# Prompt attention on TensorE: score products placed ahead of and between the groups of turned probabilities

## The reference, cut to what matters

```python
def diff_attn_prompt(q, k, v, lam):
    ...
        p1 = jax.nn.softmax(jnp.where(causal, jnp.einsum('bqhd,bkhd->bhqk', qb[..., :HEAD_DIM], k1), NEG), axis=-1)
        p2 = jax.nn.softmax(jnp.where(causal, jnp.einsum('bqhd,bkhd->bhqk', qb[..., HEAD_DIM:], k2), NEG), axis=-1)
        return jnp.einsum('bhqk,bkhd->bqhd', p1 - lam * p2, vf)
```

## Time and profile before

| | before |
|---|---|
| median of 3 runs | 2821.29 us |
| profiled execution, its own time | 2816.94 us |
| its span, first to last instruction | 2814.8 us |
| TensorE busy (matmul), whole span | 2492.6 us, 89% |
| DVE, ACT, POOL busy, whole span | 42%, 24%, 5% |
| mean granted TensorE clock | 0.942 of full |

### The profile page before, as it was taken

The page is one execution under the profiler, slowest core; times in us unless marked ns, Lnnn a source line. Parts: engine busy times, 40 slices in busy tenths (PEclk is TensorE's granted clock), DMA queues, the critical chain, the costliest instruction groups (busy, mean ns, idle before and its releaser), DMA issues.

```text
span 2814.8 us, 39064 instructions
## 1 busy us (share of the span) xinstructions
PE 2492.6 (89%) x15803; PEld 2277.5 (81%) x15803; DVE 1170.6 (42%) x2316; ACT 669.6 (24%) x1160; POOL 153.5 (5%) x186
## 2 busy tenths in 40 slices
PE   3999967778887798999999999944899999999997
PEld 2878845545554798999999999934899999999996
DVE  5312044445577561333333333499233333333225
ACT  5212122235565231111111111123211111111112
POOL 0011100014432000000000000000000000000000
PEclk6999988899998899999999999967999999999998
DMA  2322267773353100111111111011011111111001
GB/s 95 137 77 73 107 225 298 268 255 126 121 194 127 60 31 31 46 46 46 45 45 45 45 45 45 15 38 38 31 46 46 46 46 45 46 46 45 31 23 64
DMA packets 118794, 227.60 MB, mean 81 GB/s; under 512 B 6675, under 2 KB 81732, under 8 KB 116099
## 3 DMA queue, kind: packets, MB, share of 16 engines
q1 hardware_dynamic: 113267, 178.67, 18.7%
q0 software_dynamic: 5392, 46.96, 4.8%
HBM read 207.49 MB, written 51.41 MB: 92 GB/s over the span
## 4 chain that ended last, share of the span: by engine, by line
PE 77%; DVE 8%; issue 8%; ACT 2%; DMA 2%; SPq 2%; POOL 1%; DVEq 0%; ACTq 0%
PE ps L1562 69%; DMA kraw<-cache_win_k_a 2%; PE ps L1628 2%; PE ps L656 1%; PE ps L637 1%; PE ps L622 1%; ACT sm L551 1%; SPq L726 1%; DVE orms L1369 1%; POOL sm L864 1%; DVE rstd L1197 1%; DVE pa L1506 1%; SPq L723 1%; DVE sm L496 1%; PE ps L1642 1%
## 5 line engine op out<-in xcount | busy, mean ns | idle before, releaser
L1562 PE MATMUL ps<-xn,ws 128*128 128x384 f32 (+1 forms) x6912 | 1171.2, 331 | 90.0 <-issue 39.9
L1562 PEld LDWEIGHTS ps<-xn,ws 128*128 128x128 f32 x6912 | 1164.4, 191 | 95.9 <-issue 58.0
L1562 PE MATMUL ps<-hh,ws 128*128 128x384 f32 (+1 forms) x3168 | 533.9, 329 | 8.7 <-issue 8.7
L1562 PEld LDWEIGHTS ps<-hh,ws 128*128 128x128 f32 x3168 | 529.4, 189 | 9.2 <-issue 9.2
L1403 DVE TENSOR_TENSOR act_h<-act_s,ps 128x384 f32<-128x384 f32 x132 | 70.2, 532 | 901.0 <-ACT act_s L1043 901.0
L1390 DVE TENSOR_TENSOR x<-ps,x 128x384 f32<-128x384 f32 (+1 forms) x552 | 284.8, 533 | 190.8 <-PE ps L1562 189.1
L1043 ACT ACTIVATE act_s<-ps 128x384 f32<-128x384 f32 x132 | 62.5, 473 | 1261.1 <-PE ps L1562 1145.9
L1562 PE MATMUL ps<-wp,xn 128*128 128x512 f32 (+1 forms) x1296 | 297.3, 392 | 18.8 <-DVE xn L1210 18.8
L1562 PEld LDWEIGHTS ps<-wp,xn 128*128 128x128 f32 (+1 forms) x1296 | 237.5, 183 | 79.0 <-issue 19.7
L1329 DVE TENSOR_TENSOR ws<-wraw,ws 128x2048 fp32r<-128x2048 f32 x70 | 159.6, 2283 | 7.1 <-ACT ws L998 7.1
L1628 PE MATMUL ps<-ident,kraw 128*128 128x128 f32 x512 | 91.4, 333 | 60.4 <-DMA kraw<-cache_win_k_a 34.0
(11 more groups left out here) (178 smaller groups left out, 1449.0 us busy)
## 6 DMA issues: line engine op xcount, KB each, us to landing
wraw<-w_gate SPq DMA_DIRECT2D x22, 1024.0 KB, 5.2
wraw<-w_up SPq DMA_DIRECT2D x22, 1024.0 KB, 5.2
wraw<-w_down SPq DMA_DIRECT2D x22, 1024.0 KB, 4.8
kraw<-cache_win_k_a SPq DMA_DIRECT2D x8, 2048.0 KB, 8.0
vraw<-cache_win_v_a SPq DMA_DIRECT2D x8, 2048.0 KB, 11.4
kraw<-cache_k_b SPq DMA_DIRECT2D x64, 256.0 KB, 11.3
vraw<-cache_v_b SPq DMA_DIRECT2D x64, 256.0 KB, 4.2
o_wk_s<-cache_win_k_a POOLq DMA_DIRECT2D x8, 2032.0 KB, 9.0
```

The source lines that it names most:

```text
L1562: r = mm(out, w(a), m(b_), start=(i == 0 and q_ == 0), stop=(i == n - 1 and q_ == 2))
```

## The change

`scores` and `turn_p` now take a list of what to do, and the loop over the steps on TensorE puts a unit's first two score products (the first 512 keys, both halves) ahead of the turned groups, and the other two, where there are any, behind the first group (`mix` 1) or the first two groups (`mix` 0). The waits within stay as they are, and go along with what they guard. Nothing changes on the other engines.

```diff
-            def scores(u):
+            def score_pieces(u):
+
+                return [(c0, s) for c0 in range(0, unit_at(u)[3], 512) for s in range(2)]
+
+            def scores(u, pieces):
 
                 pair, mix, i, n = unit_at(u)
-                if i == 0:
+                if not pieces:
+                    return
+                if i == 0 and pieces[0] == (0, 0):
                     for part in range(2):
                         pe.wait_ge(qk_ready[part], 2 * pair + 2)
                 masked_before = 8 * pair + (0, 0, 1, 2, 4, 5, 6, 7)[i]
                 if masked_before:
                     pe.wait_ge(scores_masked, 2 * masked_before)
...
-                q_.then_inc(scores_done, 1)
-
-            def turn_p(u):
+                if pieces[-1] == score_pieces(u)[-1]:
+                    q_.then_inc(scores_done, 1)
+
+            def turn_p(u, groups):
...
-                for s, k0, cnt in turn_groups(u):
+                for s, k0, cnt in groups:
...
             for step in range(UNITS + VALUE_LAG):
+                pieces = score_pieces(step) if step < UNITS else []
+                scores(step, pieces[:2])
                 if 0 <= step - TURN_LAG < UNITS:
-                    turn_p(step - TURN_LAG)
-                if step < UNITS:
-                    scores(step)
-                    if next_round(step):
-                        turn_qk(*next_round(step))
+                    u = step - TURN_LAG
+                    groups = turn_groups(u)
+                    first = 1 if unit_at(u)[1] else 2
+                    turn_p(u, groups[:first])
+                    scores(step, pieces[2:])
+                    if groups[first:]:
+                        turn_p(u, groups[first:])
+                else:
+                    scores(step, pieces[2:])
+                if step < UNITS and next_round(step):
+                    turn_qk(*next_round(step))
```

More of the change, by code:

```diff
@@ L617, in scores @@
                     pe.wait_ge(scores_masked, 2 * masked_before)
-                for c0 in range(0, n, 512):
+                for c0, s in pieces:
                     w = min(512, n - c0)
[L620 to L623, removed]
-                q_.then_inc(scores_done, 1)
-            def turn_p(u):
+                    rows = head_rows(s)
+                    q_ = mm(ps[:, score_bank(i, s) + c0 // 512, 0:w], qk[rows, pair % 2, 0, i * P:(i + 1) * P],
+                            qk[rows, pair % 2, 1, c0:c0 + w], start=True, stop=True)
+                if pieces[-1] == score_pieces(u)[-1]:
+                    q_.then_inc(scores_done, 1)
+            def turn_p(u, groups):
                 pair, mix, i, n = unit_at(u)
```

## The result

The changed kernel has a median of 2789.81 us over 4 runs (2784.56 to 2793.64), the kernel before 2820.84 us in the same session (4 runs, 2819.74 to 2822.61). The ratio is 0.9888, with a 95% interval of 0.9871 to 0.9905: faster by 31 us, 1.1%. The forecast was 2822.3 us in a range from 2814 to 2831, so the result lies outside of it. The profiled execution took 2784.56 us, with a span of 2782.5 us and a mean granted clock of 0.954 (before 2816.94, 2814.8 and 0.942).

A forecast was written before the change was run, and what follows sets the result against it. TensorE's waits in the 287.1 us stage, for banks and masks, and its half clock were taken as the bound. +5.7 - 1.6 - 0.8 - 2.3 = +1.0 on 2816.94, plus 4.35 to the median: 2822.3 us, range 2814 to 2831.

The forecast's parts named there:

- Outside it nothing moves: Whole kernel: only the 287.1 us stage that the change touches was taken to change in time.
- Part 1, last pair: Blocks 4 to 7: 13 turned blocks and four splits inside the mask loop add 2.7 us, bounds 1.4 to 3.3.
- Part 2, pairs 4 to 6: Mix 1 pairs: +0.9 us in pairs 5 and 6, +0.3 in pair 4, and +0.3 more for each of three.
- Part 3, mix 0 pairs: Pairs 0 to 3: bank waits exchanged for mask waits, -0.4 us a pair, -1.6 for four, bounds -3 and +2.
- The mask loop: Rival, chance 0.25: the loop of scores and masks binds mix 0 pairs too, +1.3 us each, 2831.4 us in all.
- The start: First pair's start, where a block waited 2.3 us for q's copy: 0.8 us less.
- Part 4, clock: Stage: stretches at half clock fall from eight to six, -2.3 us, bounds -9.2 and +1.2.
- clock kept: Rival, chance 0.15: half-clock stretches vanish and mix 0 pairs take the better account, -7.3 us, 2814.0 us.
- A mean clock of 0.99 in the stage: Sign named against the forecast: the stage's mean granted clock, 0.95 before, goes to 0.99.
- The price of a stretch: Stage: each half-clock stretch was taken to cost 1.15 us, from a range of 0.6 to 1.4.
- slow stretches follow the long waits: Stage: half clock follows TensorE waits of 1.84, 2.06 us and the like, or two waits close together.
- The exchange of waits: Stage, chance 0.60: turned blocks' waits for q and k copies nearly vanish; scores' mask waits grow from 8.3 to over 25 us.

The follow-up runs named there:

- e1: Kernel before plus four one-column matmuls (16 TensorE instructions) in idle time ahead of layer 1's feed-forward loop, attention unchanged; 2800.44 us, ratio 0.993.
- e2: Changed kernel plus 60 one-column matmuls (240 instructions) ahead of layer 1's loop, which then stands 256 instructions behind its place before; 2815.39 us, ratio 0.9978.
- e3: Against the kernel before, all of a unit's scores ahead of all its turned groups, none between; no padding; 2806.08 us (one run).
- e6: Kernel before with all of a unit's scores ahead of its turned groups, plus 16 TensorE instructions ahead of layer 1's loop; 2786.44 us, ratio 0.9878.
- e7: Kernel before plus 32 one-column matmuls (128 TensorE instructions) ahead of layer 1's loop; 2801.46 us (one run).
- e9: Changed order in pairs 0 to 3, order of before in pairs 4 to 7, plus 16 instructions ahead of layer 1's loop; 2792.26 us (one run).
- e10: Changed kernel plus 16 TensorE instructions ahead of layer 1's loop; 2792.32 us (one run).
- e11: Changed order in pairs 0 to 3, order of before in pairs 4 to 7, plus 32 instructions ahead of layer 1's loop; 2796.71 us (one run).
- e8: Kernel before plus one one-column matmul (4 TensorE instructions) ahead of layer 1's loop; 2803.07 us (one run).
- e5: Against the changed kernel, a unit's scores whole, behind its first turned group (one or two groups, or mix 1) or second (four groups); 2762.62 us, ratio 0.9798.
- e4: Against the changed kernel, none in front: all of a unit's scores behind its first group (mix 1) or first two groups (mix 0); 2785.82 us (one run).

## Why the prediction was wrong

**"Outside it nothing moves": wrong, and this is the step that failed.** Two thirds of the gain lie in a loop that the change doesn't touch. The second call of `turn_p` repeats a wait, so that the waits don't all stay as they are, as the account of the change has it: 16 instructions more moved the loop by 16, and the gaps of 3.4 to 4 us at its returns, with the half clock behind them, went (e1: 22 us by position alone; e2: 25.6 us back). The profile of before has these gaps as "issue" waits at the returns; the prediction gives them no term, because the stage bounded what was thought to move.

The parts of the stage are compared below in pairs with equally much half clock, which takes the clock out of them.

**Part 1, last pair, +2.7: right.** 15.3 us from block 4 to block 7 (15.2 forecast), and the last pair 38.6 for 35.5, +3.1. e3 to e6, which don't split, have 35.6 to 35.8.

**Part 2, pairs 4 to 6, +3.0: right in pairs 5 and 6, too small in pair 4.** A pair 5 or 6 free of half clock went from 28.97 (e1, e7) to 30.16, +1.2, where +0.9 and +0.3 were forecast. Pair 4 free of it went from 34.1 (e1) to 35.8, +1.7, where +0.6 was forecast. Together +4.1.

**Part 3, mix 0 pairs, -0.4 each: the right sign, too small.** A pair free of half clock takes 38.42, against 39.36 (one pair, in e1), -0.9, which times four is beyond the bound of -3. Block 0 waits 1.78 us (2.05 forecast). The terms of that part also don't add up as written: its waits sum to 7.9, not 8.1. The mask loop didn't take these pairs as well, so that rival falls. The start was mis-sized: the first pair went from 34.6 to 28.4 with 6.8 and 3.4 us at half clock; e7's, with 3.4 in the order of before, takes 32.25, so 3.8 of the 6.2 us are the order's, where -0.4 and -0.8 were forecast. Together -3.8 and three times -0.9, -6.6, where -2.4 was forecast.

**Part 4, clock, -2.3: mis-sized.** Half clock in the stage went from 27.3 to 6.8 us, two stretches of 3.4 instead of eight, and not to six. By the price above that is -7 to -12, around the bound of -9.2 that the text gave to the rival "clock kept". A mean clock of 0.99 in the stage, which the prediction named as a sign against itself, is what the profile shows. The price of a stretch (1.15) was about right, since -7.8 for six fewer, as the sum below leaves it, makes 1.3; the count was not. The argument that slow stretches follow the long waits is borne out as a matter of frequency only: at the wait of 2.06 us in pairs 4 to 6 of the order of before a stretch came in 14 of 18 cases (six traces), at the new one of 1.78 in pairs with `mix` 0 in 8 of 18 (the changed kernel, e2, e9, e10, e11), and at those of 1.3 to 1.4 in pairs 5 to 7 of the changed order never (three traces). Which of them brings one is not explained.

**The exchange of waits: right.** Scores wait 35.4 us for masks (over 25 forecast), turned blocks no longer for q and k.

In the stage then: +3.1 and +4.1 for pairs 4 to 7 and -6.6 for pairs 0 to 3 make +0.6 for the order, where +3.3 was forecast; -7.2 was measured, which leaves -7.8 for the clock, where -2.3 was forecast. Between the +1.0 that was forecast for the profiled execution and its -32.4 there are thus 20.2 us in the last stretch, 8.2 in the stage (5.5 the clock, 2.7 the order) and 4.9 in the rest, for which no run shows a cause. Without the position the result would be 2815.39 (e2), inside the range at its lower end. That the order comes within 3 us of its forecast is in part luck: pairs 0 to 3 gained 4.2 us more than was said, and pairs 4 to 7 lost 1.5 more.

## What to carry to other kernels

An edit that changes the number of instructions moves all code behind it. Look at the returns of every hardware loop behind the edit, before and after, and compare at equal positions (a few instructions of padding in idle time) before a gain or a loss is put down to the edit. Here one padding matmul of four instructions took 18.7 us off the kernel before (e8, one run), where the change took 31.

In a loop of products and masks, work may stand in the mask's wait, or between two groups that wait for a bank, but not inside the products that the next mask waits for: e5 keeps the scores whole and takes 27 us off the changed kernel.

## What the runs showed of the hardware

- The same loop of 1796 recorded instructions takes 142.5 to 143.9 us or 147.5 to 149.3 us an iteration, by position. In the bad one each return waits 3.4 to 4.1 us, and 3.4 to 6.8 us at the 1.2 GHz level follow. Bad: before, +256 (e2), e3. Good: +4, +16, +32, +128.
- The number of packets on the instruction queue doesn't tell it: 36 in the loop with the gaps (before, e2), and 36 without (e7).
- A repeated wait is not always an instruction more: the 16 that the second call of `turn_p` repeats are 16 records more, those that a split of the scores repeats are none (e4, e5, e9).
- Half clock can come or not in the same order of the same stage: 6.8 and 17.1 us in two traces of one order (e3, e6), 17.1 to 27.3 in four of another. In pairs 5 and 6 it came in 9 of 12 pairs that have a wait of 2.06 us, and in none of 14 without it.
